# A hybrid attention and state-space block on one core: block-diagonal queries and a two-chunk key band for the scores, full-row value products in the first tile

## What is computed

```python
qc = q.reshape(b, n_c, CHUNK, ATTN_KV_HEADS, rep, HEAD_DIM)
...
    def band(t):
        return jnp.concatenate(
            [jnp.pad(t, ((0, 0), (sh, 0), (0, 0), (0, 0), (0, 0)))[:, :n_c] for sh in shifts], axis=2)
    kb, vb = band(kc), band(vc)
...
    scores = jnp.einsum('bcqgrd,bckgd->bcgrqk', qc, kb,
                        preferred_element_type=jnp.float32) * (1.0 / math.sqrt(HEAD_DIM))
    scores = jnp.where(valid[None, :, None, None, None, :], scores, -jnp.inf)
...
    probs = jax.nn.softmax(jnp.concatenate([scores, sink], axis=-1), axis=-1)[..., :-1]
    out = jnp.einsum('bcqgrk,bckgd->bcqgrd', probs.astype(v.dtype), vb)
```

## Time and profile before

| what | value |
|---|---|
| median of 3 runs | 1129.58 us |
| lowest, highest run | 1127.31, 1131.26 us |
| span of the profiled execution | 1130.6 us |
| mean granted TensorE clock | 0.974 of full |
| PE, PEld busy | 97%, 81% |
| DVE, ACT, POOL busy | 58%, 40%, 12% |
| transfers | 95.5 MB, 84 GB/s on average |

### The profile page before, as it was taken

One profiled execution on the slowest core, in us unless ns is written; L12 is line 12 of the kernel. 1 busy time (PEld: TensorE's weight loads), 2 busy tenths in 40 slices (PEclk: granted clock), 3 DMA queues, 4 the chain that ended last, 5 costly groups with the idle time before them and its releaser, 6 DMA issues.

```text
span 1130.6 us, 14815 instructions
## 1 busy us (share of the span) xinstructions
PE 1100.1 (97%) x5409; PEld 914.0 (81%) x5409; DVE 656.0 (58%) x943; ACT 448.7 (40%) x688; POOL 131.9 (12%) x197
## 2 busy tenths in 40 slices
PE   6999999998999999999999999989999999999997
PEld 6887888778877987788888888879888888888886
DVE  6885668573876686684343222366666666662214
ACT  5464346333463455453232213255344343431212
POOL 7012201320022102210000000220000000000001
PEclk9998999898989999899999999999999999999999
DMA  7230132012310322023224234442133242333221
GB/s 202 87 95 1 39 112 78 18 37 78 96 37 1 111 76 76 1 75 112 74 77 129 93 111 149 149 112 76 42 106 104 82 111 78 108 108 109 82 75 75
DMA packets 111608, 95.53 MB, mean 84 GB/s; under 512 B 15343, under 2 KB 101691, under 8 KB 111547
## 3 DMA queue, kind: packets, MB, share of 16 engines
q1 hardware_dynamic: 111547, 94.74, 27.7%
HBM read 92.63 MB, written 2.10 MB: 84 GB/s over the span
## 4 chain that ended last, share of the span: by engine, by line
PE 90%; DVE 3%; ACT 2%; issue 2%; DMA 1%; POOL 1%; SPq 0%; DVEq 0%; POOLq 0%; ACTq 0%
PE ps L1165 17%; PE ps L1166 17%; PE ps L1167 17%; PE ps L1172 10%; PE ps L1173 9%; PE ps L1174 9%; PE ps L1386 2%; PE ps L1331 2%; PE ps L1408 1%; PE ps L1333 1%; DVE wlo L764 1%; PE ps L1398 1%; PE ps L1382 1%; PE ps L1207 1%; PE ps L1307 1%
## 5 line engine op out<-in xcount | busy, mean ns | idle before, releaser
L764 DVE TENSOR_TENSOR wlo<-raw,whi 128x2048 fp32r<-128x2048 f32 (+1 forms) x83 | 189.1, 2280 | 224.5 <-ACT whi L433 224.5
L1165 PE MATMUL ps<-uhi,whi 128*128 128x512 f32 x640 | 249.2, 389 | 0.0
L1167 PE MATMUL ps<-uhi,wlo 128*128 128x512 f32 x640 | 249.1, 389 | 0.0
L1166 PE MATMUL ps<-ulo,whi 128*128 128x512 f32 x640 | 249.0, 389 | 0.0
L433 ACT ACTIVATE whi<-raw 128x2048 fp32r<-128x2048 f32 (+1 forms) x83 | 156.2, 1883 | 178.6 <-PE ps L1174 98.1
L1172 PE MATMUL ps<-whi,uhi 128*128 128x512 f32 (+1 forms) x320 | 129.3, 404 | 11.7 <-issue 5.9
L1167 PEld LDWEIGHTS ps<-uhi,wlo 128*128 128x128 f32 x640 | 120.2, 188 | 25.2
L1165 PEld LDWEIGHTS ps<-uhi,whi 128*128 128x128 f32 x640 | 120.1, 188 | 25.1 <-DVE wlo L764 0.2
L1166 PEld LDWEIGHTS ps<-ulo,whi 128*128 128x128 f32 x640 | 120.2, 188 | 24.4
L1173 PE MATMUL ps<-whi,ulo 128*128 128x512 f32 (+1 forms) x320 | 125.1, 391 | 0.0
L1174 PE MATMUL ps<-wlo,uhi 128*128 128x512 f32 (+1 forms) x320 | 124.9, 390 | 0.0
(11 more groups left out here) (222 smaller groups left out, 1490.9 us busy)
## 6 DMA issues: line engine op xcount, KB each, us to landing
raw<-in_w_in_dram SPq DMA_DIRECT2D x24, 1024.0 KB
raw<-in_w_up_dram SPq DMA_DIRECT2D x44, 512.0 KB
raw<-in_w_down_dram SPq DMA_DIRECT2D x11, 1024.0 KB
raw<-in_w_in_dram SPq DMA_DIRECT2D x16, 512.0 KB
raw<-in_w_ssd_out_dram SPq DMA_DIRECT2D x8, 1024.0 KB
raw<-in_w_attn_out_dram SPq DMA_DIRECT2D x4, 1024.0 KB
raw<-in_w_out_dram SPq DMA_DIRECT2D x4, 1024.0 KB
yT<-in_x_dram SPq DMA_DIRECT2D x4, 512.0 KB, 5.2
```

What stands on the lines that cost most here:

```text
L764: dve.tensor_tensor(wlo[sl][:, 0:width] if into is None else into, raw[sl][:, 0:width], h.bitcast(F32), ALU.subtract).then_inc(s["lo_done" ...
L1165: pe.matmul(bank(b)[:, span], hi_[:, k, c], ah[:, span], start=first and k == 0, stop=False)
L1166: pe.matmul(bank(b)[:, span], hi_[:, k, c], al[:, span], start=False, stop=False)
L1167: ins = pe.matmul(bank(b)[:, span], lo_[:, k, c], ah[:, span], start=False, stop=last and k == KD - 1)
```

## The change

`qT` (two heads to a 128-row tile) becomes `qB`, one tile of 128 rows a head: the upper 64 rows hold the head's channels for the first chunk of each pair and zero for the second, the lower 64 rows the other way round. `kT` becomes `kB`: the lower rows hold the keys as before; the upper rows hold a tile's first chunk in its own place, and in the second place the second chunk of the tile before. One matmul over 128 rows then gives all four blocks of a head's scores. GpSimd writes the zeros once, at the start, with three memsets and a semaphore `band_zero`. ACT writes `qB` with eight copies (two heads, two halves of rows, twice) and `kB` with three, in place of three copies in all. The value products of tile 0 always use 128 rows; the upper rows of `va` for tile 0 are zeroed.

```diff
@@ -109,8 +109,8 @@
         qk_rot = sb("qk_rot", [P, NT, QW + 2 * KW], where=gctx)
         rtmp = sb("rtmp", [P, QW + KW], where=gctx)
         va = sb("va", [P, NT + 1, HD], where=gctx)
-        qT = sb("qT", [P, 2, S], where=gctx)
-        kT = sb("kT", [P, S], where=gctx)
+        qB = sb("qB", [P, QH, S], where=gctx)
+        kB = sb("kB", [P, S], where=gctx)
         conv = sb("conv", [P, 6, S], where=gctx)
         tanh_c = sb("tanh_c", [P, 2, S], where=gctx)
         b_tok = sb("b_tok", [P, S], where=gctx)
@@ -157,7 +157,7 @@
-            "dve_chain", "pool_chain", "xsq", "rstd",
+            "band_zero", "dve_chain", "pool_chain", "xsq", "rstd",
 ...
@@ -332,6 +332,13 @@
 
             for t in range(NT):
                 root_x(t)
+
+            pool.memset(qB[:, :, :], 0.0).then_inc(s["band_zero"], 1)
+            pool.wait_ge(s["band_zero"], 1)
+            pool.memset(kB[0:HD, HD:P], 0.0).then_inc(s["band_zero"], 1)
+            pool.wait_ge(s["band_zero"], 2)
+            pool.memset(va[HD:P, 0, :], 0.0).then_inc(s["band_zero"], 1)
+            pool.wait_ge(s["band_zero"], 3)
 
             w0, w1 = tanh_c[:, 0, :], tanh_c[:, 1, :]
             NA = NT * HALF
@@ -543,10 +550,23 @@
                 tap(4)
                 tanh(3)
                 tap(5)
-                for j in range(3):
+                def halves(a):
+                    return a.rearrange("p (t b c) -> p t b c", b=2, c=HD)
+
+                act.wait_ge(s["band_zero"], 3)
+                up_, dn_ = slice(0, HD), slice(HD, P)
+                for j in range(2):
                     act.wait_ge(s["qkT_mm"], G * 3 + (j + 1))
-                    act.activation(qT[:, j, :] if j < 2 else kT[:, :], bank(j), ACT.Copy,
-                                   scale=HD ** -0.5 if j < 2 else 1.0).then_inc(s["qkT_sb"], 1)
+                    for a, r in ((0, up_), (1, dn_)):
+                        for b, d in ((0, up_), (1, dn_)):
+                            ins = act.activation(halves(qB[d, 2 * j + a, :])[:, :, b, :], halves(ps[r, j, :])[:, :, b, :],
+                                                 ACT.Copy, scale=HD ** -0.5)
+                    ins.then_inc(s["qkT_sb"], 1)
+                act.wait_ge(s["qkT_mm"], G * 3 + 3)
+                act.activation(kB[dn_, :], ps[dn_, 2, :], ACT.Copy)
+                act.activation(halves(kB[up_, :])[:, :, 0, :], halves(ps[up_, 2, :])[:, :, 0, :], ACT.Copy)
+                act.activation(halves(kB[up_, :])[:, 1:, 1, :], halves(ps[up_, 2, :])[:, 0:NT - 1, 1, :],
+                               ACT.Copy).then_inc(s["qkT_sb"], 1)
                 act.wait_ge(s["decay_mm"], G + 1)
                 act.activation(dec[:, :, :, :].rearrange("p a t h -> p (a t h)"), bank(3, 3 * NT * SH), ACT.Exp).then_inc(s["decay_ok"], 1)
                 tok(0)
@@ -1326,12 +1346,8 @@
                         else:
                             pe.wait_ge(s["conv_ok"], G * 6 + 6)
                         for h in range(QH):
-                            r = slice((h % 2) * 64, (h % 2) * 64 + 64)
                             b, o = 4 + h % 2, (h // 2) * P
-                            ins = pe.matmul(ps[:, b, o:o + P], qT[r, h // 2, c], kT[r, c], start=True, stop=True)
-                            if t:
-                                ins = pe.matmul(ps[0:64, b, o + 64:o + P], qT[r, h // 2, t * P:t * P + 64],
-                                                kT[r, t * P - 64:t * P], start=True, stop=True)
+                            ins = pe.matmul(ps[:, b, o:o + P], qB[:, h, c], kB[:, c], start=True, stop=True)
                         ins.then_inc(s["s_mm"], 1)
 
                     def turn_p():
@@ -1403,9 +1419,8 @@
                         r = slice((h % 2) * 64, (h % 2) * 64 + 64)
                         for half in (1, 0):
                             o = ps[r, 4, (h // 2) * P + 64 * half:(h // 2) * P + 64 * half + 64]
-                            n = 64 if t == 0 and half == 0 else P
-                            v = qkv_sb[0:n, t, QW + KW:QW + 2 * KW] if half else va[0:n, t, :]
-                            ins = pe.matmul(o, v, pT[0:n, (h % 2) * 2 + h // 2, 64 * half:64 * half + 64], start=True, stop=True)
+                            v = qkv_sb[:, t, QW + KW:QW + 2 * KW] if half else va[:, t, :]
+                            ins = pe.matmul(o, v, pT[:, (h % 2) * 2 + h // 2, 64 * half:64 * half + 64], start=True, stop=True)
                     ins.then_inc(s["o_mm"], 1)
 
             with pe.Fori(0, NG // 2) as i:
```

More of the change, by code:

```diff
@@ L159, in hybrid_block @@
             "x_in0", "x_in1", "x_in2", "x_in3", "consts_in", "par_in", "par2_in", "posT_ok", "pool_c", "loaded0", "loaded1", "hi_done", "lo_done", "blk_done",
-            "dve_chain", "pool_chain", "xsq", "rstd", "xn", "xT_mm", "u_plain", "uhi_ok", "u_ok", "u2_ok", "parT_mm", "par_ok",
+            "band_zero", "dve_chain", "pool_chain", "xsq", "rstd", "xn", "xT_mm", "u_plain", "uhi_ok", "u_ok", "u2_ok", "parT_mm", "par_ok",
             "ang_ok", "rope_tab", "params_ok", "hp_ok",
```

## The result

The median fell from 1128.44 us (4 runs, 1126.91 to 1131.26) to 1098.28 us (4 runs, 1096.58 to 1099.32). The ratio is 0.973, with a 95% interval of 0.9709 to 0.9751: 30 us, or 2.7%, faster. The forecast was 1091.5 us in a range of 1085 to 1106. The direction and the range held; the time came out 7 us above the forecast.

The account below looks back on a forecast made before the run. The matmul engine, busy 97% of the span, was taken as the bound. -22.6 - 5.6 - 18.8 + 7.2 + 1 + 0.5 = -38.3 us from the profiled 1130.6 gave 1092.3, about 1091.5 as median, range 1085 to 1106.

Parts of the forecast that it names:

- part 1: Scores in tiles 1 to 3: eight 128-row records take 0.87 us, gaining 1.88 us a tile, 22.6 us in all.
- about 1 us of slack is left: VectorE's path from scores to `xdt` against PE's in tile 2; 1 us in all put on it for 12 tiles.
- part 2: Value products in tile 0: full rows cut 2.07 us to 0.66, 1.41 us a group, 5.6 us in all.
- part 3: PE's clock in the tiles: no stretch with 64 rows is left, so it stays up, gaining 18.8 us.
- rival B: Clock still falls twice a group, as the page's rule has it; the 18.8 us are gone: 1110 us, chance 0.08.
- part 4: ACT's evictions ahead of tile 0: eleven copies for three add 1.8 us a group, 7.2 us in all.
- Rival A: One clock fall per group stays or comes anew, costing 7 to 12 us: 1099 to 1103 us, chance 0.20.
- part 5: Start of the kernel: GpSimd's memset ahead of the angles makes later work slide, adding 0.5 us.

Follow-up runs that it names:

- the later wait: Changed kernel with PE's waits for the masked decays and `xdt` moved behind the state product: 1094.31 us, ratio 0.9715.
- the kernel with the wide matmuls: Kernel before with full-row value products in tile 0 and the first score matmul over all 128 rows: 1106.29 us, ratio 0.9817.
- the regrouped scores: Kernel before with full-row value products in tile 0, all heads' 128-wide score matmuls first, then the 64-wide ones: 1088.56 us, ratio 0.9656.
- the three copies: Changed kernel with one 128-row ACT copy per bank, leaving out the block form and two heads' queries: 1085.59 us, ratio 0.9636.
- the later kernels without the early memset: Changed kernel with memsets behind GpSimd's input part: 1096.36 us; the same with four query copies and PE's waits behind the state product: 1090.87 us.

## Why the prediction was right, and where it was off

**Scores, part 1.** Right in kind and, by PE, in size: 0.81 to 0.89 us a tile were forecast as 0.87. The step that failed is "about 1 us of slack is left". It let PE do the state product before it reads `xdt`; in the code the wait for `xdt` stands ahead of the state product, and the 0.86 us of L1382 were no slack. VectorE sets the pace of tile 2 at 13.35 us, where PE needs 12.77 (the later wait shows it). The shorter scores were worth about 20 us instead of 21.6: 19.1 against the kernel with the wide matmuls, and the 1 us that this one had already.

**Value products, part 2.** Forecast 5.6, measured 5.7.

**The clock, part 3.** Forecast 18.8; between the profiles the kernel with wide matmuls and full-row value products puts it at about 18. Between medians it is less: that kernel lies 20.2 us below its before, and less the 5.7 of the value products and the 1 of its shorter scores some 13.5 are left. The profile of before that the term was read from had an uncommonly low clock. The reason given, rows at work and not gaps, is shown for the second fall, which goes when only rows change. It isn't the whole of it. I let each fall follow its own stretch, and the first needed two, the slow value products and the long scores behind them; there full rows in the first score matmul took it away in one group of four. And the regrouped scores, 64 rows but short, bring no fall. So the rows count together with how long such a stretch lasts, and what exactly the clock follows stays open.

The Trainium skill's page "TensorE: Matmul & The Clock Gate", section "Why this matters for your kernels", ties the loss of clock to gaps between bursts. By that rule rival B's 1110 would have come. The runs speak against it as the only cause: the second fall came with PE busy throughout, and it went when the rows of one matmul changed and its place in time hardly did.

**The evictions, part 4.** Right that all of it lies on the chain, which the three copies show. Mis-sized: 0.28 us a copy was taken from 128-row neighbours, and 64-row ones that change the half of the rows each time stand 0.376 apart. The term is 10.7 us, not 7.2, inside the bounds of 4 to 12. The estimate by the Trainium skill's page "ScalarE: Activation LUTs", section "What ACT_TABLE_LOAD costs", with its overlap of 93 ns, was 8 us. It misses for the same reason: these copies did not overlap.

**Rival A in small.** PE's three waits, 2.2 us together in group 0, brought a fall ahead of tile 0 in three groups; with three copies both are gone. The price was 0.9 us in all and not 7 to 12: from `dec` to the second half of z it is 8.01 to 8.29 us in the groups with a fall and 7.73 in the one without. The z block's rest on DVE is ready only 0.6 us before PE reaches it, and hides most of the fall.

**The start, part 5.** +0.7 in the profiles against 0.5, but this is luck: it compares with a start that had a fall of its own. Against the later kernels without the early memset, which have none, it is 2.5 us and more. I had looked at what waits for GpSimd and not at what runs beside it.

**The sum.** Forecast -38.3, between the profiles -35.1, between the medians -30.2. The terms missed by 6.6 us together: evictions 3.5, scores and their slack 1.6, the fall ahead of tile 0 0.9, the clock 0.5, the rest 0.1. That the profiles come within 3.2 us is luck, for "all else" gave 3.4 that nothing in the change accounts for. The last 5 us are the choice of reference: the profiled execution of before lies 4.0 us above its median, that of the changed kernel 1.0 below.

## What to carry to other kernels

Before giving small matmuls full rows by copies, look at the order in which their forms alternate: grouping equal forms, with full rows for the value products, gave here a better time than the change did (1088.6 us against 1098.3), with no new copy. A matmul engine that is called busy can still lose its clock behind a long stretch in which few rows work, and what follows then pays too: here that was as much as the stretches themselves. And work taken off PE at the price of copies on another engine pays in full only where the chain does not run through that engine.

## What the runs showed of the hardware

- Alternating matmuls of 64 rows by 128 columns with ones of 64 by 64 took 0.67 us a head; the same ones grouped took 0.26. With 128 by 128 in place of the first kind the alternation took 0.67 too. The Trainium skill's page "TensorEngine Tiling (Array Packing)", section "Tiling Modes", under "Key Properties", says that a change of tiling mode drains the engine; these numbers agree.
- The granted clock fell to half (0.50, 3.4 us in each group) right behind score stretches of 2.7 us whose matmuls all had 64 rows, with PE busy throughout. It stayed at 1.00 behind stretches of 2.6 us whose first matmul of each pair had 128 rows, and behind 64-row stretches of 1.0 us. Behind slow value products those 128 rows did not suffice in three groups of four.
- Three waits of PE of 0.41, 0.92 and 0.84 us among short matmuls were followed by 3.4 us of half clock in three groups of four; without the waits there was none in any group.
- ACT copies of 64 rows by 256 columns that wrote the two halves of the rows in turn stood 0.376 us apart; two that wrote the same half stood 0.28 apart, and copies of 128 rows 0.29.
- A scaling on VectorE of 128 by 1024 took 2.27 us beside a GpSimd memset and 0.75 without. It began 0.08 us behind the memset and ended 0.55 us behind it, as if it had stood still for most of the memset's 1.80. The Trainium skill's page "SBUF — State Buffer", section "Who interferes with whom", has the two engines share a pair of ports that the first to come keeps for its whole instruction, where the VectorE instruction runs in a mode that uses both; these times agree with it.
